# Modulation sums of the first quarter on TensorE in 32-column tiles, and the second half of the features in two quarters

## The chip, the cores and the metric

One core of a Trainium2 chip runs the whole program. The metric is the device time in microseconds (us) of one execution. The kernel before was timed in three runs: 2482.34, 2482.88 and 2483.24 us, median 2482.88.

## The reference, cut to what matters

Three transformer-like layers over 256 tokens of 2048 features, in float32. Only the head of the first one is touched:

```
mod = silu(c) @ ada_w + ada_b            # c: 2048, ada_w: 2048 x 6144
shift, scale, gate = split(mod, 3)
h = rms_norm(x, norm_g) * (1 + scale) + shift
proj = h @ w_in                          # 256 x 2048 by 2048 x 9296
...
x = x + gate * mix
```

So no product of `h` can start before the shift and the scale of its features are there, and these are sums over all 2048 rows of a 50 MB matrix.

## The kernel before, in words

**Products.** Every large product runs over slabs: a slab is 1 MB of weights (two blocks of 128 rows by 1024 columns), fetched in two halves of 512 KB by SyncE's queue into one of five `raw` slots (RING = 5), rounded by ScalarE to `hi` (four slots, L1206) and completed by VectorE with `lo = raw - hi` (L1753). TensorE takes three passes for each block (hi·h_hi, lo·h_hi, hi·h_lo; L642 to L644), 24 matmuls of 512 columns for each slab. In what follows p0, p1, ... are the products of slabs 0, 1, ...; the order is a list written out by hand (`slabs`, L287 on), and every engine walks it in its own loop over m. SyncE fetches slab m when p(m-5) is done. Features are blocks of 128, 16 in all. p0 to p7 use blocks 0 to 3 (the first quarter), p8 to p15 blocks 4 to 7 (the second), p16 to p23 blocks 0 to 7 again for two other column groups, p24 to p27 blocks 8 to 15 (two to a slab), p28 and p29 are small ones over all 16. In step m of the loops over the front (L1385, L2060) ScalarE and VectorE first hand over finished PSUM banks, then convert slabs up to m + 3 (`conv_to(m + 3)`), and then do whatever else is put at that step.

**Modulation.** `ada_w` comes in 48 slabs a of 1 MB: a = 0 to 7 and 8 to 15 hold the shift and the scale columns of the first and the second quarter, 16 to 23 the shift columns of the second half, 24 to 31 its scale columns, 32 to 47 the gate's. VectorE multiplies each by silu(c) and adds it to a row of 1024 sums on every partition, two instructions a slab (L1729, L1732); slab 1 alone is taken by TensorE, by 16 matmuls with one moving column (L786). When eight slabs are summed, TensorE sums over the partitions and turns the result into columns by matmuls against a column of ones (`quarter_columns` L768, `ada_columns` L743), VectorE adds bias and gain (`quarter_scales` L1829, `modulation` L1820), ScalarE writes `h_raw` and `h_hi` (L1251, L1253) and VectorE `h_lo` (L1817), two feature blocks in one `split_modulated(i)`; it raises `h_ready` by 2, and a product waits for `h_ready` up to its last block.

**Order of the sums.** `conv(m)` of VectorE first does the ada slabs up to `ada_until(m)` (L307, L1762): for m from 8 to 24 one slab to each step, so that the last one (a = 31) stands ahead of conv(24), and a gate slab ahead of conv(25), conv(26), conv(27), ... The columns of the second half are made inside p21 and p22, its scales in VectorE's step 22 (T_COLS), `split_modulated(4)` and `(5)` in step 22, `(6)` and `(7)` in step 23. POOL's queue fetches a from 13 on, each when VectorE is done with an earlier one (L2506), and a = 0 to 12 stand in SyncE's queue between the first slabs (L550 to L571).

**Start.** x (2 MB) comes by ScalarE's queue; its normalised rows xn are turned by TensorE (`turn_xn`, L755), four times four blocks ahead of the first columns and four times four behind them, ahead of p0.

Of the kernel before, what the change touches and what calls it, by code (L numbers as in the profile page):

```python
# [12 lines left out]
P = 128  # L13
# [81 lines left out]
def build(nc, t_in, out):  # L95
# [33 lines left out]
    def slot(i):  # L129
        return G0 + 8 * i  # L130
# [4 lines left out]
    gate = at("gate", [P, D], slot(7))  # L135
    ada_sum = [gate[:, 0:GW], gate[:, GW:D], tmp1, tmp2, gate[:, 0:GW], gate[:, GW:D]]
    ang = at("ang", [P, 4, TT * 96], G0 + 83)
# [160 lines left out]

    ADA_COLS = (0, HALF, GW, D + GW, 2 * D, 2 * D + GW)
    N_ADA, N_MOD, N_QUARTER, N_START = 48, 32, 8, 16  # L300
    PE_ADA = (1,)

# [4 lines left out]
    def ada_until(m):  # L307
        gates = sum(t <= m for t in GATE_AT)
        return N_MOD + gates if gates else (6, 8, 10, 11, 12, 13, 14, 15)[m] if m < 8 else min(N_START + m - 8, N_MOD)

# [203 lines left out]
    def ada_part(a, part):  # L514

        k, c = 2 * (a % 8) + part, ADA_COLS[a // 8]
        dst = ada_slot(a)[:, part * GW:(part + 1) * GW]
        if a >= N_START:
            return ada_w[k * P:(k + 1) * P, c:c + GW], dst
        both = ada_w[k * P:(k + 1) * P, 0:2 * D].rearrange("p (e n) -> p e n", e=2)  # L520
        return both[:, :, c:c + HALF], dst.rearrange("p (e n) -> p e n", e=2)
# [6 lines left out]
    def _(sp):  # L528
# [23 lines left out]
        for m in range(N_SLABS):  # L552
# [9 lines left out]
            if m == 3:  # L562
                sp.wait_ge(xn_ready, 2)
                ada_fetch(10, quarter_landed[2])
                sp.wait_ge(ada_added, added(7))
                ada_fetch(11, early_landed[2])
            if m == 4:
                sp.wait_ge(ada_added, added(8))
                ada_fetch(12, early_landed[3])
# [23 lines left out]
    def _(pe):  # L593
# [146 lines left out]

        columns_made = [0]

        def ada_columns():  # L743


            e, half = columns_made[0] // 2, columns_made[0] % 2
            pe.wait_ge(ada_added, added(8 * (2 + e + 1)))
            for k in range(4 * half, 4 * half + 4):
                ins = pe.matmul(wk[:, 2 + e, k:k + 1], ada_sum[2 + e][:, k * P:(k + 1) * P], ones[:, 0:1],
                                start=True, stop=True)  # L750
            if half:
                ins.then_inc(ada_turned, 1)
            columns_made[0] += 1

        def turn_xn(i):  # L755
# [11 lines left out]

        def quarter_columns(block, banks, start):  # L768

            pe.wait_ge(ada_added, added(8 * (block + 1)))  # L770
            for pair in range(2):
                for e in range(2):
                    for f in (2 * pair, 2 * pair + 1):
                        ins = pe.matmul(quarter_col(banks, e, f), ada_sum[block][:, e * HALF + f * P:e * HALF + (f + 1) * P],
                                        ones[:, 0:1], start=start, stop=True, skip_group_check=not start)
                ins.then_inc(ada_turned, 1)

        pe.wait_ge(c_silu, 1)
        pe.wait_ge(gains_out, 1)
        for a in PE_ADA:  # L780
            ada_wait(pe, a)
            for e in range(2):
                for f in range(4):
                    for part in range(2):
                        b = part * GW + e * HALF + f * P
                        ins = pe.matmul(quarter_col(acc, e, f), ada_slot(a)[:, b:b + P], c_col[:, 2 * a + part:2 * a + part + 1],  # L786
                                        start=a == PE_ADA[0] and f % 2 == 0 and part == 0, stop=False, skip_group_check=True)
            ins.then_inc(ada_taken, 1)
        pe.wait_ge(xn_ready, TT)
        for i in range(4):  # L790
            turn_xn(i).then_inc(turned, 1)
        quarter_columns(0, acc, False)
        for i in range(4, 8):
# [3 lines left out]
        def second_columns():  # L797

            pe.wait_ge(xn_parked, 8)
            quarter_columns(1, wk, True)  # L800

# [129 lines left out]
        for m in range(N_FRONT):  # L931
            if m == T_SECOND:
                product(*slabs[m], (0,))
                second_columns()
                product(*slabs[m], (1,))
            else:
                product(*slabs[m], range(TT), ada_columns if m in (T_COLS - 1, T_COLS) else None)
            if m == T_IK - 1:
# [252 lines left out]
    def _(act):  # L1191
# [51 lines left out]
        def split_modulated(i):  # L1243

            act.wait_ge(xn_parked, i + 1)
            act.wait_ge(mod_ready, (1, 2, 3, 4, 5, 5, 5, 5)[i])
            if i >= 2:
                act.wait_ge(h_ready, 2 * (i - 1))
            for k in (2 * i, 2 * i + 1):
                src = xnT[:, :, k, :]  # L1250
                act.activation(h_raw[:, k % 4].rearrange("p (t c) -> p t c", t=TT), src, ACT.Identity,  # L1251
                               bias=sh[:, k:k + 1], scale=gs[:, k:k + 1])
                act.activation(h_hi[:, :, k, :], src, ACT.Identity,  # L1253
                               bias=sh[:, k:k + 1], scale=gs[:, k:k + 1]).then_inc(h_hi_made, 1)
# [130 lines left out]
        for m in range(N_FRONT):  # L1385
# [21 lines left out]
            if m == T_LB + 1:  # L1407
                act.wait_ge(lb_ready, 1)
                act.activation(lb_col[:], lb_col[:], ACT.Exp).then_inc(lb_exp, 1)
            if m in (T_COLS, T_COLS + 1):  # L1410
                i = 4 + 2 * (m - T_COLS)
                split_modulated(i)
                split_modulated(i + 1)
# [296 lines left out]
    def _(vec):  # L1710
# [108 lines left out]

        def modulation():  # L1820

            c, shift_cols, scale_cols, signal = slice(8, 16), wk[:, 2, 0:8], wk[:, 3, 0:8], 5
            vec.wait_ge(ada_turned, signal)
            step(vec.tensor_tensor(sh[:, c], shift_cols, gcols[:, B_SHIFT, c], ALU.add))
            vec.wait_ge(ada_turned, signal + 1)
            step(vec.tensor_tensor(gs[:, c], scale_cols, gcols[:, B_SCALE, c], ALU.add))
            vec.tensor_tensor(gs[:, c], gs[:, c], gcols[:, N_MIX, c], ALU.mult).then_inc(mod_ready, 1)

        def quarter_scales(q, pair, banks):  # L1829

            vec.wait_ge(ada_turned, 2 * q + pair + 1)
            c = slice(4 * q + 2 * pair, 4 * q + 2 * pair + 2)
            vec.tensor_tensor(sh[:, c], banks[:, 2 * pair, 0:2], gcols[:, B_SHIFT, c], ALU.add)
            for f in range(2):
                k = 4 * q + 2 * pair + f
                ins = vec.tensor_scalar(gs[:, k:k + 1], banks[:, 2 * pair + 1, f:f + 1], gcols[:, B_SCALE, k:k + 1],
                                        gcols[:, N_MIX, k:k + 1], ALU.add, ALU.mult)
            ins.then_inc(mod_ready, 1)
# [6 lines left out]


        vec.wait_ge(rows_turned, 1)
        vec.tensor_copy(c_col[:], acc[:, 1, 0:KT]).then_inc(cols_out, 1)
        step(vec.tensor_copy(lb_col[:], acc[:, 1, KT:2 * KT]))
        vec.wait_ge(c_silu, 1)  # L1850
        ada_to(1)
        vec.wait_ge(rows_turned, 2)
# [207 lines left out]
        for m in range(N_FRONT):  # L2060
# [550 lines left out]
```

## Time and profile before

| | us |
|---|---|
| median of three runs | 2482.88 |
| the profiled execution | 2482.34 |
| its span in the trace | 2480.5 |
| TensorE matmul busy | 2435.8 (98%) |
| VectorE busy | 1625.9 (66%) |
| ScalarE busy | 1190.5 (48%) |
| DMA | 507 MB, 204 GB/s on average |

The profiled execution is 1.8 us longer than its span, and 0.5 us below the median. An engine's share is its busy time over the span. In the first fortieth (62 us) TensorE is busy for half of the time, in all the others for at least nine tenths; over the first 150 us the DMA engines move about 380 GB/s, later about 190.

### The profile page before, as it was taken

The numbers are of one execution on the slowest core, as the hardware profiler recorded it, in microseconds if no ns is written. First come the engines' busy times: TensorE is split into PE (matmuls) and PEld (weight loads), VectorE is DVE, ScalarE is ACT, GpSimd is POOL, SyncE is SP. The second block draws the span as 40 slices with busy tenths as digits, with TensorE's granted clock in tenths as the row PEclk, the third lists the DMA queues.
The fourth block names the chain that finished last, engine by engine and source line by source line (L and its number), as shares of the span: only waits on it lengthen the run. The fifth ranks groups of instructions, "written<-read, shape, count | busy, mean of one in ns | idle before, by whom it ended". The sixth has DMA issues, their size and how long they took to land.

```text
span 2480.5 us, 28566 instructions
## 1 busy us (share of the span) xinstructions
PE 2435.8 (98%) x11262; PEld 2016.7 (81%) x11262; DVE 1625.9 (66%) x2086; ACT 1190.5 (48%) x1549; POOL 110.1 (4%) x158
## 2 busy tenths in 40 slices
PE   5999999999999999999999999999999999999998
PEld 4888778888788888888888888888888888888887
DVE  6987988756776675764445655765676766754444
ACT  4756666445544444444343544554544444444332
POOL 1210000000100000000000212000000000000000
PEclk9999999999999999999999999999999999999999
DMA  9997655564565655656555655446565655656553
GB/s 385 364 365 245 238 187 171 180 244 153 171 199 190 194 197 188 200 190 207 197 190 190 193 195 180 154 146 207 174 200 188 196 194 189 200 188 208 197 189 135
DMA packets 189492, 507.04 MB, mean 204 GB/s; under 512 B 17792, under 2 KB 18080, under 8 KB 188080
## 3 DMA queue, kind: packets, MB, share of 16 engines
q1 hardware_dynamic: 177008, 456.92, 55.0%
q0 software_dynamic: 11824, 46.14, 5.0%
q8 instruction: 90, 1.47, 0.2%
q10 hardware_dynamic: 528, 2.16, 0.2%
q14 instruction: 42, 0.34, 0.0%
HBM read 503.06 MB, written 2.10 MB: 204 GB/s over the span
## 4 chain that ended last, share of the span: by engine, by line
PE 94%; DVE 4%; ACT 1%; issue 1%; DMA 1%; SPq 0%; DVEq 0%; ACTq 0%
PE acc L642 30%; PE acc L644 30%; PE acc L643 30%; DVE lo L1753 1%; DVE gate L1732 1%; PE wk L665 1%; DVE lo L1755 1%; DMA raw<-in_ada_w 1%; ACT hi L1206 0%; PE wk L1128 0%; PE wk L1154 0%; PE wk L826 0%; PE wk L1115 0%; PE wk L865 0%; PE wk L840 0%
## 5 line engine op out<-in xcount | busy, mean ns | idle before, releaser
L642 PE MATMUL acc<-hi,h 128*128 128x512 f32 x2592 | 1018.8, 393 | 3.6 <-ACT kiT L1322 1.5
L644 PE MATMUL acc<-hi,h 128*128 128x512 f32 x2592 | 1009.6, 390 | 0.0
L643 PE MATMUL acc<-lo,h 128*128 128x512 f32 x2592 | 1009.1, 389 | 0.0
L1755 DVE SCALAR_TENSOR_TENSOR lo<-raw,gcols,hi 128x1024 fp32r<-128x1024 f32 (+1 forms) x464 | 572.9, 1278 | 200.3 <-ACT hi L1206 198.3
L1206 ACT ACTIVATE hi<-raw,gcols 128x1024 fp32r<-128x1024 f32 (+1 forms) x464 | 497.4, 1128 | 361.5 <-PE acc L644 320.2
L1753 DVE TENSOR_TENSOR lo<-raw,hi 128x1024 fp32r<-128x1024 f32 (+1 forms) x388 | 453.5, 1213 | 301.3 <-ACT hi L1206 300.6
L642 PEld LDWEIGHTS acc<-hi,h 128*128 128x128 f32 x2592 | 486.8, 188 | 106.9 <-issue 5.4
L644 PEld LDWEIGHTS acc<-hi,h 128*128 128x128 f32 x2592 | 486.6, 188 | 102.0
L643 PEld LDWEIGHTS acc<-lo,h 128*128 128x128 f32 x2592 | 487.0, 188 | 98.9 <-issue 0.2
L1206 ACT ACTIVATE hi<-raw 128x1024 fp32r<-128x1024 f32 (+1 forms) x388 | 384.9, 1045 | 348.2 <-DMA raw<-in_w_ffn_down 164.7
L642 PE MATMUL acc<-hi,g_hi 128*128 128x512 f32 x704 | 274.2, 389 | 0.0
L644 PE MATMUL acc<-hi,g_lo 128*128 128x512 f32 x704 | 273.9, 389 | 0.0
L643 PE MATMUL acc<-lo,g_hi 128*128 128x512 f32 x704 | 273.9, 389 | 0.0
L644 PEld LDWEIGHTS acc<-hi,g_lo 128*128 128x128 f32 x704 | 132.1, 188 | 27.6
L642 PEld LDWEIGHTS acc<-hi,g_hi 128*128 128x128 f32 x704 | 132.1, 188 | 27.5
L643 PEld LDWEIGHTS acc<-lo,g_hi 128*128 128x128 f32 x704 | 132.2, 188 | 27.0
L2340 DVE STREAM_TRANSPOSE g_raw<-gated 32x256 f32<-32x256 f32 x320 | 139.6, 436 | 5.9
L2330 DVE SCALAR_TENSOR_TENSOR gated<-acc,stats,gated 128x512 f32<-128x512 f32 x44 | 33.0, 750 | 142.2 <-PE acc L644 142.2
L1598 ACT ACTIVATE gated<-acc,stats 128x512 f32<-128x512 f32 x44 | 30.3, 689 | 143.1 <-PE acc L644 143.1
L1232 ACT ACTIVATE h<-wk 128x512 fp32r<-128x512 f32 x44 | 24.4, 593 | 50.8 <-PE wk L665 50.4
L1800 DVE TENSOR_TENSOR h<-wk,h 128x512 fp32r<-128x512 f32 x44 | 28.8, 685 | 30.0 <-ACT h L1232 29.8
L1611 ACT ACTIVATE g_hi<-g_raw 128x512 fp32r<-128x512 f32 x40 | 23.1, 625 | 49.6 <-DVE g_raw L2340 49.6
(327 smaller groups left out, 1225.1 us busy)
## 6 DMA issues: line engine op xcount, KB each, us to landing
raw<-in_w_ffn_gate SPq DMA_DIRECT2D x176, 512.0 KB, 3.8
raw<-in_w_ffn_up SPq DMA_DIRECT2D x176, 512.0 KB, 4.6
raw<-in_w_ffn_down SPq DMA_DIRECT2D x176, 512.0 KB, 4.8
raw<-in_w_in SPq DMA_DIRECT2D x144, 512.0 KB, 4.7
raw<-in_w_kv SPq DMA_DIRECT2D x64, 512.0 KB, 4.8
ada_raw<-in_ada_w POOLq DMA_DIRECT2D x38, 512.0 KB, 7.7
gate_raw<-in_ada_w POOLq DMA_DIRECT2D x32, 512.0 KB, 5.6
raw<-in_w_out SPq DMA_DIRECT2D x32, 512.0 KB, 5.0
```

The source lines that it names most:

```text
L642: pe.matmul(o, l_hi, w_hi[:, c], start=first, stop=False, skip_group_check=loaded)
L643: pe.matmul(o, l_hi, w_lo[:, c], start=False, stop=False, skip_group_check=loaded)
L644: mm = pe.matmul(o, l_lo, w_hi[:, c], start=False, stop=last, skip_group_check=loaded)
L665: ins = pe.transpose(wk[:, i % 4, kk * P:(kk + 1) * P], block_of(4 * q + kk, t), ident[:])
L1206: ins = act.activation(hi[:, m % HI_SLOTS, c], raw[:, r, c], ACT.Copy, scale=scale)
L1598: act.activation(gated[:, t, :], acc[:, st.bank(t, 0), :], ACT.Silu, scale=rstd[:, t:t + 1]).then_inc(acc_free[st.bank(t, 0)], 1)
L1732: ins = vec.scalar_tensor_tensor(out=dst[:], in0=src, scalar=c_col[:, k:k + 1], in1=dst[:], op0=ALU.mult, op1=ALU.add)
L1753: ins = vec.tensor_tensor(lo[:, r, c], raw[:, r, c], hi[:, m % HI_SLOTS, c], ALU.subtract)
L1755: ins = vec.scalar_tensor_tensor(out=lo[:, r, c], in0=raw[:, r, c], scalar=gcols[:, st.gain, k:k + 1], in1=hi[:, m % HI_SLOTS, c], op0=ALU ...
L1800: vec.tensor_tensor(part_lo[:, t, k, :], wk[:, i % 4, :].rearrange("p (k c) -> p k c", k=4), part_hi[:, t, k, :], ALU.subtract).then_inc(h ...
L2330: vec.scalar_tensor_tensor(out=gated[:, t, :], in0=acc[:, st.bank(t, 1), :], scalar=rstd[:, t:t + 1], in1=gated[:, t, :], op0=ALU.mult, op ...
L2340: ins = vec.transpose(dst, src)
```

## The change

TensorE sums a = 0 to 7. silu(c) is written into column 0 of 16 groups of 32 columns of zeros (`c_pad`); for each ada slab four matmuls of 128 rows, 32 stationary and 512 moving columns go to the four 32-column tiles of the array, so that the four pieces (shift and scale of two row blocks) land on partitions 0, 32, 64 and 96 of one PSUM bank and accumulate over the eight slabs. ScalarE copies the bank (`ada_rows`), and four matmuls against a 0/1 selector of two columns make the columns of shift and scale. Slabs 0 to 4 come ahead of the first four turns of xn, slabs 5 to 7 behind them. VectorE has no ada slab before a = 8.

The second half is split as the first was: a = 16 to 23 hold shift and scale of blocks 8 to 11, a = 24 to 31 those of blocks 12 to 15 (fetched as 2 x 512 columns where it was 1024). Their columns are made in p21 and in p23, 8 matmuls each (before: 16 in p21 and p22); the scales stand in VectorE's steps 22 and 24; `split_modulated(4)`, `(5)` in step 22, `(6)`, `(7)` in step 24, behind conv(27). From m = 16 on `ada_until` is one slab lower: nothing ahead of conv(16), a = 30 ahead of conv(24), a = 31 and 32 ahead of conv(25).

```diff
+    c_pad = at("c_pad", [P, KT, 32], slot(7))
+    ada_rows = at("ada_rows", [P, HALF], slot(7) + 2)
-    ADA_COLS = (0, HALF, GW, D + GW, 2 * D, 2 * D + GW)
+    ADA_COLS = (0, HALF, 2 * HALF, 3 * HALF, 2 * D, 2 * D + GW)
-    PE_ADA = (1,)
+    PE_ADA = tuple(range(N_QUARTER))
@@ ada_until
-        return N_MOD + gates if gates else (6, 8, 10, 11, 12, 13, 14, 15)[m] if m < 8 else min(N_START + m - 8, N_MOD)
+        return N_MOD + gates if gates else (8, 8, 10, 11, 12, 13, 14, 15)[m] if m < 8 else min(N_START + m - 8 - (m >= N_START), N_MOD)
@@ SyncE, m == 3 and m == 4
-                sp.wait_ge(ada_added, added(7))
+                wait_summed(6)
-                sp.wait_ge(ada_added, added(8))
+                wait_summed(7)
@@ TensorE
+        def pair_columns(block, banks, pair):
+            pe.wait_ge(ada_added, added(8 * (block + 1)))
+            if block == 3:
+                pe.wait_ge(mod_ready, 5 + pair)
+            for e in range(2):
+                for f in (2 * pair, 2 * pair + 1):
+                    ins = pe.matmul(quarter_col(banks, e, f), ada_sum[block][:, e * HALF + f * P:e * HALF + (f + 1) * P],
+                                    ones[:, 0:1], start=True, stop=True)
+            ins.then_inc(ada_turned, 1)
...
+        def ada_row_sums(a):
+            ada_wait(pe, a)
+            for j in range(4):
+                ins = pe.matmul(acc[32 * j:32 * j + 32, 3, :], c_pad[:, 2 * a + j // 2, :],
+                                ada_slot(a)[:, j * HALF:(j + 1) * HALF], start=a == 0, stop=a == N_QUARTER - 1)
+            ins.then_inc(ada_taken, 1)
+        def first_columns():
+            pe.wait_ge(rows_out, 1)
+            pe.wait_ge(sel_ready, 1)
+            for pair in range(2):
+                for f in range(2):
+                    c = 2 * pair + f
+                    ins = pe.matmul(acc[:, 2 * pair, 2 * f:2 * f + 2], ada_rows[:, c * P:(c + 1) * P], sel,
+                                    start=True, stop=True)
+                ins.then_inc(ada_turned, 1)
-        for a in PE_ADA:
...
+        for a in range(5):
+            ada_row_sums(a)
         pe.wait_ge(xn_ready, TT)
         for i in range(4):
             turn_xn(i).then_inc(turned, 1)
-        quarter_columns(0, acc, False)
+        for a in range(5, N_QUARTER):
+            ada_row_sums(a)
+        first_columns()
@@ front loop
-                product(*slabs[m], range(TT), ada_columns if m in (T_COLS - 1, T_COLS) else None)
+                product(*slabs[m], range(TT), pairs_of(2 + (m > T_COLS)) if m in (T_COLS - 1, T_COLS + 1) else None)
@@ ScalarE
-            act.wait_ge(mod_ready, (1, 2, 3, 4, 5, 5, 5, 5)[i])
+            act.wait_ge(mod_ready, i + 1)
+        act.activation(c_pad[:, :, 0], c_col[:], ACT.Silu)
+        act.wait_ge(ada_taken, N_QUARTER)
+        act.activation(ada_rows[:], acc[:, 3, :], ACT.Copy).then_inc(rows_out, 1)
-            if m in (T_COLS, T_COLS + 1):
-                i = 4 + 2 * (m - T_COLS)
+            if m in (T_COLS, T_COLS + 2):
+                i = 4 + m - T_COLS
@@ VectorE
-        ada_to(1)
-        ada_to(3)
-        ada_to(N_QUARTER)
-            if m == T_COLS:
-                modulation()
-            if m in (T_SECOND - 2, T_COLS, T_COLS + 1):
-                i = 2 if m == T_SECOND - 2 else 4 + 2 * (m - T_COLS)
+            if m in (T_COLS, T_COLS + 2):
+                q = 2 + (m > T_COLS)
+                quarter_scales(q, 0, wk)
+                quarter_scales(q, 1, wk)
+            if m in (T_SECOND - 2, T_COLS, T_COLS + 2):
+                i = 2 if m == T_SECOND - 2 else 4 + m - T_COLS
```

## Rows read from the trace of the kernel before

**Rows 1.** Busy time by stretch: us, PE, PEld, DVE, ACT, POOL, PEclk, DMA share, GB/s.
```profile
0.00:45.00 45.00, 17.54 (x79) 16.69 (x80) 24.54 (x40) 16.97 (x20) 0.20 (x4) 1.00 0.97 374
45.00:80.00 35.00, 35.00 (x155) 29.07 (x154) 34.03 (x30) 22.87 (x34) 11.05 (x18) 1.00 1.02 391
...
260.00:2480.00 2220.00, 2206.95 (x10202) 1824.90 (x10201) 1410.82 (x1815) 1030.99 (x1297) 75.41 (x92) 1.00 0.57 189
```

**Rows 2.** Timeline, 38 to 47 us: start, duration, engine, line, [idle before].
```profile
38.85 3.57 PE L774 MATMUL acc<-ones,gate 128*128 128x1 f32 x16 [8.09 <-DVE gate L1732]
40.75 0.16 DVE L1833 TENSOR_TENSOR sh<-acc,gcols 128x2 f32<-128x2 f32 x1 [1.96 <-PE acc L774]
...
42.28 3.65 PE L760 MATMUL wk<-ident,xn 128*128 128x128 f32 x16
...
43.55 0.69 DVE L1817 TENSOR_TENSOR h<-h_raw,h 128x512 fp32r<-128x512 f32 x1 [0.56 <-ACT h L1253]
...
45.59 0.78 PE L642 MATMUL acc<-hi,h 128*128 128x512 f32 x1
```

**Rows 3.** SyncE's issue of early_raw, and its time to landing.
```profile
DMA to landing us min/median/max: 10.6/11.6/12.6
```

**Rows 4.** Timeline of TensorE around other float32 matmuls.
```profile
447.21 1.99 PE L894 MATMUL wk<-r_qe,r_e 128*32 128x64 f32 x128
537.01 3.60 PE L1011 MATMUL wk<-gate,ones 128*128 128x512 f32 x8
164.47 0.95 PE L749 MATMUL wk<-ones,tmp 128*128 128x1 f32 x8
```

**Rows 5.** Timeline of ScalarE, where it waited for slabs 4 and 7.
```profile
59.56 2.01 ACT L1206 ACTIVATE hi<-raw 128x1024 fp32r<-128x1024 f32 x2 [1.75 <-DMA raw<-in_w_in]
74.84 2.01 ACT L1206 ACTIVATE hi<-raw 128x1024 fp32r<-128x1024 f32 x2 [3.28 <-DMA raw<-in_w_in]
```

**Rows 6.** Timeline of VectorE and POOL, 48 to 88 us.
```profile
48.02 0.75 DVE L1729 TENSOR_SCALAR gate<-ada_raw,c_col 128x1024 f32<-128x1024 f32 x1
50.39 1.60 POOL L2509 DMA_DIRECT2D ada_raw<-in_ada_w  x2 [49.95 <-DVE gate L1732]
...
76.64 2.35 DVE L1753 TENSOR_TENSOR lo<-raw,hi 128x1024 fp32r<-128x1024 f32 x2
...
87.92 0.16 DVE L1833 TENSOR_TENSOR sh<-wk,gcols 128x2 f32<-128x2 f32 x1 [0.53 <-PE wk L774]
```

**Rows 7.** Timeline of VectorE, 159 to 198 us.
```profile
159.45 2.36 DVE L1753 TENSOR_TENSOR lo<-raw,hi 128x1024 fp32r<-128x1024 f32 x2 [0.52 <-ACT hi L1206]
...
171.30 2.60 DVE L1732 SCALAR_TENSOR_TENSOR gate<-gate_raw,c_col,gate 128x1024 f32<-128x1024 f32 x2
173.81 2.35 DVE L1753 TENSOR_TENSOR lo<-raw,hi 128x1024 fp32r<-128x1024 f32 x2
...
186.63 2.36 DVE L1753 TENSOR_TENSOR lo<-raw,hi 128x1024 fp32r<-128x1024 f32 x2 [2.27 <-ACT hi L1206]
189.61 0.69 DVE L1817 TENSOR_TENSOR h<-h_raw,h 128x512 fp32r<-128x512 f32 x1 [0.62 <-ACT h L1253]
...
192.20 2.60 DVE L1732 SCALAR_TENSOR_TENSOR gate<-gate_raw,c_col,gate 128x1024 f32<-128x1024 f32 x2
194.72 2.35 DVE L1753 TENSOR_TENSOR lo<-raw,hi 128x1024 fp32r<-128x1024 f32 x2
```

**Rows 8.** Timeline of ScalarE, 177 to 186 us.
```profile
177.00 0.60 ACT L1251 ACTIVATE h_raw<-xnT,sh,gs 128x256 f32<-128x256 f32 x1 [2.97 <-issue]
...
180.96 0.57 ACT L1313 ACTIVATE proj<-acc 128x512 f32<-128x512 f32 x1
...
185.55 1.99 ACT L1206 ACTIVATE hi<-raw 128x1024 fp32r<-128x1024 f32 x2
```

**Rows 9.** Issues of SyncE's queue at the ends of p22 and p25.
```profile
177.97 0.98 SPq L582 DMA_DIRECT2D raw<-in_w_in  x2
...
194.32 0.81 SPq L582 DMA_DIRECT2D raw<-in_w_in  x2
```

More of the change, by code:

```diff
@@ L135, in build @@
     gate = at("gate", [P, D], slot(7))
-    ada_sum = [gate[:, 0:GW], gate[:, GW:D], tmp1, tmp2, gate[:, 0:GW], gate[:, GW:D]]
+    ada_sum = [None, gate[:, GW:D], tmp1, tmp2, gate[:, 0:GW], gate[:, GW:D]]
+    c_pad = at("c_pad", [P, KT, 32], slot(7))
+    ada_rows = at("ada_rows", [P, HALF], slot(7) + 2)
     ang = at("ang", [P, 4, TT * 96], G0 + 83)
@@ L220, in build @@
     ssd, dstd = stats[:, 160:176], stats[:, 176:192]
+    sel = stats[:, 250:252]
     lam_s, lam_e, nlam = stats[:, 192:194], stats[:, 194:196], stats[:, 196:197]
@@ L373, in build @@
     ada_added, ada_turned, mod_ready = sem("ada_added"), sem("ada_turned"), sem("mod_ready")
+    pad_clear, sel_ready, rows_out = sem("pad_clear"), sem("sel_ready"), sem("rows_out")
     hi_made = sem("hi_made")
@@ L517, in ada_part @@
         dst = ada_slot(a)[:, part * GW:(part + 1) * GW]
-        if a >= N_START:
+        if a >= N_MOD:
             return ada_w[k * P:(k + 1) * P, c:c + GW], dst
@@ L739, in _ @@
         pe.transpose(acc[:, 0, 0:P], rows[:], ident[:]).then_inc(rows_turned, 1)
[L741 to L753, printed above, removed]
         def turn_xn(i):
@@ L766, in quarter_col, with pairs_of, fill, quarter_columns @@
             return banks[:, b, f % 2:f % 2 + 1]
-        def quarter_columns(block, banks, start):
+        def pair_columns(block, banks, pair):
             pe.wait_ge(ada_added, added(8 * (block + 1)))
-            for pair in range(2):
[L772 to L775, printed above, removed]
+            if block == 3:
[5 more added lines that the diff above has]
+            ins.then_inc(ada_turned, 1)
+        def pairs_of(block):
+            left = [0, 1]
+            def fill():
+                pair_columns(block, wk, left.pop(0))
+            return fill
+        def quarter_columns(block, banks):
+            for pair in range(2):
+                pair_columns(block, banks, pair)
+        def ada_row_sums(a):
[12 more added lines that the diff above has]
+                                    start=True, stop=True)
                 ins.then_inc(ada_turned, 1)
@@ L779, in _ @@
         pe.wait_ge(gains_out, 1)
-        for a in PE_ADA:
[L781 to L788, printed above, removed]
+        for a in range(5):
+            ada_row_sums(a)
         pe.wait_ge(xn_ready, TT)
@@ L799, in second_columns @@
             pe.wait_ge(xn_parked, 8)
-            quarter_columns(1, wk, True)
+            quarter_columns(1, wk)
         fills = []
@@ L1270, in _ @@
         act.wait_ge(cols_out, 1)
+        act.wait_ge(pad_clear, 1)
+        act.activation(c_pad[:, :, 0], c_col[:], ACT.Silu)
         act.activation(c_col[:], c_col[:], ACT.Silu).then_inc(c_silu, 1)
@@ L1818, in split_modulated @@
                               h_hi[:, :, k, :], ALU.subtract).then_inc(h_ready, 2)
[L1820 to L1827, printed above, removed]
         def quarter_scales(q, pair, banks):
@@ L1832, in quarter_scales @@
             c = slice(4 * q + 2 * pair, 4 * q + 2 * pair + 2)
-            vec.tensor_tensor(sh[:, c], banks[:, 2 * pair, 0:2], gcols[:, B_SHIFT, c], ALU.add)
+            if q:
+                shift_cols, scale_cols = banks[:, 2 * pair, 0:2], banks[:, 2 * pair + 1, 0:2]
+            else:
+                by_kind = banks[:, 2 * pair, 0:4].rearrange("p (f e) -> p e f", e=2)
+                shift_cols, scale_cols = by_kind[:, 0, :], by_kind[:, 1, :]
+            vec.tensor_tensor(sh[:, c], shift_cols, gcols[:, B_SHIFT, c], ALU.add)
             for f in range(2):
                 k = 4 * q + 2 * pair + f
-                ins = vec.tensor_scalar(gs[:, k:k + 1], banks[:, 2 * pair + 1, f:f + 1], gcols[:, B_SCALE, k:k + 1],
+                ins = vec.tensor_scalar(gs[:, k:k + 1], scale_cols[:, f:f + 1], gcols[:, B_SCALE, k:k + 1],
                                         gcols[:, N_MIX, k:k + 1], ALU.add, ALU.mult)
@@ L1844, in row_scale @@
             vec.sem_inc(rstd_ready, 1)
+        vec.memset(c_pad[:], 0.0).then_inc(pad_clear, 1)
+        for j in range(4):
+            for e in range(2):
+                ins = vec.memset(sel[32 * j:32 * j + 32, e:e + 1], float(e == j % 2))
+        ins.then_inc(sel_ready, 1)
         vec.wait_ge(rows_turned, 1)
@@ L1849, in _ @@
         step(vec.tensor_copy(lb_col[:], acc[:, 1, KT:2 * KT]))
-        vec.wait_ge(c_silu, 1)
-        ada_to(1)
         vec.wait_ge(rows_turned, 2)
@@ L1860, in _ @@
         vec.sem_inc(rstd0_ready, 1)
+        vec.wait_ge(c_silu, 1)
         conv_to(0)
-        ada_to(N_QUARTER)
         quarter_scales(0, 0, acc)
```

## The prediction

> **What bounds the kernel now.** I read the busy time by stretch first, then TensorE's waits, then the timelines at the two places that the change touches. TensorE is the bound from 45 us on: 35.0 of 35.0 us busy to 80 us, 2207 of 2220 us behind 260 us [rows 1]. So a gain can come from the first 45 us alone, where it works for 17.5 us, and from there on the change can only keep the gain or lose it. Two things run close behind TensorE in 45 to 80 us: the DMA engines (share 1.02, 391 GB/s: full) and VectorE (34.0 of 35.0 us) [rows 1]. What ends last at the start is VectorE's sum: the first columns wait 8.1 us for it, begin at 38.85, the first pair reaches VectorE at 40.75, h_lo of the first blocks is done at 44.24, and p0 begins at 45.59, behind 16 turns of 3.65 us [rows 2].
>
> **The change, part by part.** The sum runs in the clock of the profiled execution of before: span 2480.5 us, its time 2482.34, 1.8 us around the span; the median of the runs is 0.5 us above that time.
>
> *Row sums.* Slab 7's last half is the last issue of its group, at 22.9 us, and lands 10.6 to 11.6 us later [rows 3]: about 33.7. VectorE has then still to do 5 us. A 512-column float32 matmul runs as two instructions of 0.43 us (eight in 3.60 us, less the last one's tail of 0.6) [rows 4]. Four of them one after the other are 3.4 us for a slab, while a slab lands every 2.6 us; all four tiles at once are 0.86 us. For the tiles the trace has a row: 64 products in 32-column tiles, 128 instructions of 64 and 32 columns, take 1.99 us [rows 4]. At 0.84 ns a column they would take 5.2 us in single file, so nearly three run at a time. Of the clock: eight one-column instructions take 0.95 us at 164 us, but 16 of them 3.57 us at 38.85 [rows 2, 4], so TensorE is at 1.2 GHz before p0 and at 2.4 after it, whatever the clock column says there. I take 1.7 us for a slab at the lower level, 0.9 at the upper. Slabs 5 to 7 stand behind turns that end at about 31.3: done at 34.7 (upper) to 36.4 (lower), I take 35.5. Then 0.6 for ScalarE's copy, 0.45 to 0.9 for the first pair of columns, 0.2 of handing over: VectorE has them at 36.9 where it was 40.75, 3.8 us earlier (2.9 to 4.9). The memsets, the second Silu and the selector lie ahead of the first landing and cost nothing; without that cover they are under 1 us. p0 gains 3.5 to 5.
>
> The Trainium skill, page "TensorE: Matmul & The Clock Gate", section "Part 3: Packing small matmuls", says that matmuls start and end in strict program order. A float32 product is two instructions on one tile here, and the second must wait for the first; in strict order every neighbour would then overlap by one instruction only, and a slab would be 4 x 0.43 = 1.7 us (3.4 at the lower clock). The 128 instructions of [rows 4] would be 2.6 us in that order and took 1.8 without the tail, so the trace speaks against it; what it would cost is a rival below.
>
> *What is left of it at p8.* Behind the start two chains must come earlier too. VectorE works without a pause from 48.02 to 87.4, then waits 0.5 us for the second quarter's columns [rows 6]. Its work is the same as before, so it can only come as early as its inputs. Slabs 4 and 7 are converted the moment they land, 59.56 and 74.84 [rows 5]: the DMA engines are full and the same bytes must pass first. From a landing it takes VectorE 3.4 us to the end of that slab's lo (1.0 for the first half of hi, 2.4 for lo), and from the end of lo 7 (78.99) to the scales 8.4 us [rows 6]. So the scales can't come before 74.8 + 3.4 + 8.4 = 86.6, where they came at 87.92. Slab 4 may even land later, since POOL's first fetch (50.39) waits for VectorE's a = 8 and so moves 3.8 us ahead into the same full engines: one more half slab, 1.3 us, ahead of slab 4 gives 86.9. TensorE has been ahead meanwhile and waits at p8 for h. Of the 3.5 to 5 us, 1.0 to 1.3 are left: I take 1.1. The bounds are 0 (slab 4 later by another microsecond) and 4.8 (landings move along).
>
> *Second half.* Here in the clock of before, the 1.1 taken off at the end. Total work on TensorE is equal: 16 products of two instructions, 3.8 us, before and after. Removing one ada slab ahead of conv(16) puts VectorE 2.5 us ahead; but at conv(22) it already waited 0.52 us for ScalarE [rows 7], so there the lead ends in a longer wait. Ahead of conv(25) stand now a = 31 and a = 32: 171.30 + 2.5 + 2.5, conv(25) 176.3 to 178.7, first scales 179.3; before, ScalarE could start on them at 177.0 [rows 7, 8]. Costs:
> - p23 began just ahead of the issue at 177.97 [rows 9]; now 1.9 us earlier (two bursts of 0.95 have left p22 [rows 4]), at 175.9, and comes to its first columns at 177.3. They wait for `mod_ready` 5, at 179.3: 2 us, with all of p23 queued behind. With the columns' own 1.9 and 5.45 of product, p24 begins at 185.3 (two products of 5.45 ahead of 194.1 before, 183.2).
> - ScalarE: splits 4 and 5 from 179.4 to 183.3, the hand-over of p23's banks 4.6 us (180.96 to 185.55 before) [rows 8], hi 26 from 187.9.
> - VectorE: lo 26 followed hi by 1.1 (186.63) [rows 7, 8], now 189.0 to 191.4. And here is the dear step: before, split 6 came straight behind it, at 189.61, done at 190.3. Now step 24 puts the gate slab (2.5) and conv(27) (2.35) first [rows 7], then the scales (0.6), then ScalarE's four activations (2.0, as 177.0 to 179.0), then h_lo (0.8): 191.4 + 2.5 + 2.4 + 0.6 + 2.0 + 0.8 = 199.7.
> - p26 needs blocks 12 and 13. Before it began at 194.1, just ahead of the issue at 194.32 [rows 9]; TensorE is there at 185.3 + 2 x 5.45 = 196.2 and waits 3.5 us, to 199.7.
>
> So p26 begins 5.6 us late. The bounds: 4.0 if VectorE keeps its lead to conv(24), 6.5 if a gate slab lands late as well. After p26 everything hangs on TensorE again and VectorE has time to spare, so I count nothing as won back; the low bound of that is 1.5 us.
>
> Sum: 2480.5 - 1.1 + 5.6 = 2485.0 of span, 2486.8 with what lies around it; from the median, 2482.88 + 4.5 = 2487.4. That is slower, by just under 0.2% (5.0 us), which is about what a measurement of this kernel tells from no change.
>
> **The rivals.**
> - *The start's gain lives.* If slabs 4 to 7 land as much earlier as TensorE runs ahead, 4.8 less remain against 5.6: 2483.7. For it: each of these fetches is issued at the end of a product. Against it: the full engines [rows 1]. Chance 0.15.
> - *Not slower.* The second half costs nothing, because the scales of the last quarter come before TensorE wants them. It decides at h_lo of blocks 12 and 13: by 194.1 on this clock, 5.6 us earlier than in my chain. Then 1.1 are won, 2481.8, or 4.8 with the rival above, 2478.1. For it: p24 and p25 give 10.9 us of cover. Against it: the chain of rows above has no slack in it. Chance 0.15, of which 0.05 for over 0.2% faster.
> - *Tiles in program order, at the lower clock.* Slabs 5 to 7 then end at 31.3 + 10.2 = 41.5, the scales come 2.7 us later than before, and all behind them: 2482.88 + 2.7 + 5.6 = 2491.2. Chance 0.12.
> - *The clock falls in the new waits.* Before, no long wait follows p0 (13 us idle in all behind 260 us [rows 1]); now TensorE waits some 2.4 us at p8 and 3.5 at p26. If the clock drops, the next products run at half speed: between 0.7 us (as long as it lasted at 45.59) and one slab's 5.4: 2488 to 2493. Chance 0.08. The Trainium skill, same page, section "Why this matters for your kernels", advises to keep long idle gaps out between bursts for this reason; no row here shows a fall after such a wait.
>
> **How the numbers follow.** The forecast has 0.50; its own range is 2484.5 to 2489.5 (start 0 to 1.5 kept, second half 4.0 to 6.5). Slower by over 0.2%, above 2487.9: 0.16 of the forecast, 0.11 of the tiles, 0.07 of the clock, 0.34. Faster by over 0.2%: 0.05. Within: 0.61. The range reaches down through the kept gain and part of the third case, and up to the tiles' lower end: 2480.5 to 2490.5.
>
> **What would show it.** Row sums of 0.9 to 1.8 us a slab, the last done by 36.4; 3.4 or more would be the tiles in order. First scales at 36 to 38, p0 at about 41. Slab 4 landing at 59.5 to 61. A wait of TensorE for ScalarE or VectorE at about 88, and the second quarter's scales at 86.5 to 87.5. A wait of 1.5 to 2.5 us at p23's first columns, on VectorE's scales. A wait of 2.5 to 4.5 us at p26 on h_lo, right behind conv(27) and split 6 of VectorE. If the waits at p8 and p26 are both missing, the forecast is wrong; with p8's alone missing it is too slow by 3.7 us.

## The result, and the profile after

| | before | after |
|---|---|---|
| median of six runs, us | 2483.47 (2482.34 to 2484.08) | 2497.03 (2496.04 to 2498.59) |
| profiled execution, us | 2482.34 | 2498.59 |
| its span, us | 2480.5 | 2496.8 |

The ratio is 1.0056, with an interval of 1.0044 to 1.0067. The change makes the kernel 13.6 us slower; 4.5 were forecast, and the time lies above the range. The page of the changed kernel, engines (busy us, share of the span, instructions):

```profile
PE 2446.3 (98%) x11286; PEld 2012.9 (81%) x11286; DVE 1611.0 (65%) x2090; ACT 1191.1 (48%) x1551; POOL 116.6 (5%) x158
```

TensorE is busy 10.5 us longer than before (2435.8): 1.4 us of that lie ahead of p0, where it has taken over VectorE's sums, and 9.1 between p0 and p28, where its work is the same. The table has the start of each product on TensorE, after minus before:

| p0 | p1 | p2 | p3 | p4 | p5 to p22 | p23 | p24 | p26 | p27 |
|---|---|---|---|---|---|---|---|---|---|
| -5.2 | -5.7 | -1.1 | +1.9 | +5.8 | +8.4 | +6.5 | +13.9 | +16.1 | +16.2 |

So the start is won (5.7 us at p1), lost again with 8.4 more by p5, and the second half adds 7.8. The changed kernel's timeline where the first columns are made (start, duration, engine, line, [idle before <- releaser]); it answers to [rows 2]. The first two lines are the row sums of one slab each, at the lower and at the upper clock by their lengths; the clock column has no record ahead of 31.3 us:

```profile
26.59 1.93 PE L786 MATMUL acc<-early_raw,c_pad 128*32 128x512 f32 x8 [3.14 <-DMA early_raw<-in_ada_w]
...
34.33 1.07 PE L786 MATMUL acc<-early_raw,c_pad 128*32 128x512 f32 x8 [0.69 <-DMA early_raw<-in_ada_w]
36.75 0.16 DVE L1851 TENSOR_TENSOR sh<-acc,gcols 128x2 f32<-128x2 f32 x1 [6.82 <-PE acc L797]
...
40.35 0.47 PE L646 MATMUL acc<-hi,h 128*128 128x512 f32 x1 [1.39 <-issue]
```

The first scales come at 36.75 where they came at 40.75. Next the changed kernel's busy time by stretch (columns as in [rows 1]; the seventh group is the granted clock):

```profile
0.00:45.00 45.00, 24.12 (x126) 11.56 (x127) 11.29 (x39) 21.81 (x30) 0.20 (x4) 1.00 0.96 372
45.00:80.00 35.00, 26.85 (x94) 21.07 (x93) 25.94 (x22) 15.82 (x21) 10.36 (x16) 0.80 0.96 360
56.00:62.00 6.00, 6.00 (x14) 4.68 (x15) 3.22 (x3) 1.23 (x3) 3.81 (x7) 0.50 1.02 417
72.00:79.00 7.00, 5.33 (x13) 4.20 (x14) 6.83 (x6) 6.77 (x10) 1.44 (x2) 0.52 0.67 267
188.00:195.00 7.00, 7.00 (x23) 5.84 (x24) 3.86 (x6) 6.31 (x13) 0.00 (x0) 0.52 0.42 167
```

And the same stretch of the kernel before, for the third of these lines:

```profile
56.00:62.00 6.00, 6.00 (x28) 4.96 (x27) 5.93 (x6) 3.06 (x4) 4.12 (x7) 1.00 1.03 420
```

From 45 to 80 us TensorE now stands for 8.2 us (35.00 - 26.85), where it had no idle time. In three stretches, two of them here and one at 188 us, it runs at 1.2 GHz (0.50 to 0.52 of the full clock): in 56 to 62 us it is busy all the time and does 14 instructions where it did 28. What it stood for in the first 400 us (waits: engine, line, releaser, us in total, times, longest):

```profile
PE acc L646 <- ACT proj L1335: 8.2, 2, 4.4
PE acc L646 <- DVE h L1839: 2.1, 1, 2.1
PE wk L765 <- DVE gs L1854: 2.1, 1, 2.1
```

The first line is the surprise: ScalarE's hand-over of finished banks (`proj`). Its timeline in the changed kernel shows why:

```profile
53.29 2.00 ACT L1224 ACTIVATE hi<-raw 128x1024 fp32r<-128x1024 f32 x2 [6.14 <-DMA raw<-in_w_in]
55.20 2.04 ACT L1335 ACTIVATE proj<-acc 128x512 f32<-128x512 f32 x4
...
65.22 2.01 ACT L1224 ACTIVATE hi<-raw 128x1024 fp32r<-128x1024 f32 x2 [7.99 <-DMA raw<-in_w_in]
...
71.04 2.00 ACT L1224 ACTIVATE hi<-raw 128x1024 fp32r<-128x1024 f32 x2 [3.81 <-DMA raw<-in_w_in]
72.95 2.04 ACT L1335 ACTIVATE proj<-acc 128x512 f32<-128x512 f32 x4
```

ScalarE works in order: it stands 6.1 us for slab 3 with the hand-over of p1's banks behind that conversion, and 8.0 and 3.8 us for slabs 4 and 5 with the hand-over of p3's banks behind them. TensorE's side of it, in the timeline:

```profile
55.92 0.76 PE L646 MATMUL acc<-hi,h 128*128 128x512 f32 x1 [4.41 <-ACT proj L1335]
```

The chain of waits, 50 to 75 us, tells the same of p4 (start, duration, step):

```profile
47.17 23.85 DMA raw<-in_w_in
72.00 1.04 ACT hi L1224
73.05 0.49 ACT proj L1335
73.67 0.76 PE acc L646
```

Slab 4 landed at 65.2, before at 59.56 [rows 5]. Slab 3 was late too, by 1.0 us (53.27 and 52.25). POOL's first fetches were issued at 46.41 (before 50.39 [rows 6]). Bytes by DMA queue from 52 to 55 us (packets, MB, share of the 16 engines), in the changed kernel, where q0 is POOL's queue and q1 carries SyncE's:

```profile
q0 software_dynamic: 225, 0.79, 64.8%
q1 hardware_dynamic: 229, 0.45, 38.5%
```

and in the kernel before:

```profile
q1 hardware_dynamic: 412, 1.14, 94.8%
q0 software_dynamic: 31, 0.13, 10.3%
```

Over 49 to 58 us (three such windows) SyncE's queue moved 0.84 + 0.45 + 0.47 = 1.76 MB after, 1.21 + 1.14 + 0.62 = 2.97 before. POOL's moved 1.98 MB after and 0.74 before, 1.24 more. The 1.21 MB that SyncE's queue is short of take 5.9 us at 205 GB/s, an estimate from the 0.61 to 0.66 MB in 3 us that this queue moves from 58 to 64 us, beside POOL's, in both kernels: slab 4's 5.7 us.

The two queues sent nearly equal numbers of packets (225 and 229; 211 and 213 from 55 to 58 us; 180 and 180 from 58 to 61), from 52 to 55 us POOL's of 3.5 KB and SyncE's of 2.0 KB, so POOL had 64% of the bytes there, though SyncE had issued slab 4's fetch at 43.9 us and POOL its first one at 46.4. The Trainium skill, page "DMA: Bandwidth & Descriptors", section "Queues, rings and completion order", says that each DMA engine goes round its queues packet by packet; the trace agrees, with those counts of its own packets. That SyncE's fetch was the older one did not help it here.

### The profile page after: what moved, and what is told of

Read it like the earlier page. It is cut to its first block, busy times and chain, and to the rows that moved or that the text cites. A ratio compares the mean times of both kernels' runs of the same rounds, so it can differ in the third digit from the quotient of the medians.

```text
span 2496.8 us, 28618 instructions
## 1 busy us (share of the span) xinstructions
PE 2446.3 (98%) x11286; PEld 2012.9 (81%) x11286; DVE 1611.0 (65%) x2090; ACT 1191.1 (48%) x1551; POOL 116.6 (5%) x158
## 4 chain that ended last, share of the span: by engine, by line
PE 92%; DVE 4%; DMA 1%; ACT 1%; SPq 1%; issue 1%; DVEq 0%; ACTq 0%
PE acc L646 29%; PE acc L648 29%; PE acc L647 29%; DVE lo L1775 1%; DMA raw<-in_w_in 1%; PE wk L669 1%; DVE lo L1777 1%; SPq L552 1%; ACT hi L1224 1%; DMA early_raw<-in_ada_w 0%; PE wk L1146 0%; PE wk L1172 0%; DVE tmp L1754 0%; PE wk L844 0%; SPq L586 0%
## 5 line engine op out<-in xcount | busy, mean ns | idle before, releaser
L1335 ACT ACTIVATE proj<-acc 128x512 f32<-128x512 f32 x55 | 32.1, 595 | 34.2 <-PE acc L648 32.3
```

The lines of the kernel that those rows point to most:

```text
L1335: act.activation(proj[:, FIRST_SEGS[4 + g if st is st_first else g], t, n * HALF:(n + 1) * HALF], o, ACT.Copy).then_inc(acc_free[b], 1)
```

## The experiments

Edits are against the changed kernel unless another is named; each was timed against the kernel before on its own chip (before: 2483.21 for e1 to e4, 2483.33 for e5 to e8, 2483.5 for e9 to e11). Starts of products are the experiment's profile minus that of before.

| | median us (range) | ratio, interval | p2 | p5 | p9 | p22 | p26 |
|---|---|---|---|---|---|---|---|
| e1_start_only | 2490.12 (2489.20 to 2490.55) | 1.0025, 1.0015 to 1.0036 | +0.3 | +7.7 | +7.7 | +7.7 | +7.7 |
| e2_second_only | 2491.14 (2488.95 to 2492.12) | 1.0030, 1.0018 to 1.0041 | +0.5 | +0.5 | +2.3 | +2.3 | +8.4 |
| e3_start_hold | 2484.78 (2483.36 to 2485.43) | 1.0005, 0.9996 to 1.0015 | -1.7 | +1.0 | +2.3 | +2.3 | +2.3 |
| e4_start_order | 2486.92 (2486.23 to 2488.90) | 1.0015, 1.0006 to 1.0025 | -4.4 | +6.3 | +6.3 | +6.3 | +6.3 |
| e5_start_hold_order | 2481.70 (2480.99 to 2483.52) | 0.9994, 0.9985 to 1.0003 | -4.8 | -4.8 | -0.9 | -1.1 | -1.1 |
| e6_after_warm | 2499.17 (2496.97 to 2499.44) | 1.0060, 1.0045 to 1.0075 | -0.1 | +8.2 | +8.2 | +8.2 | +13.8 |
| e7_second_nolag | 2488.55 (2485.56 to 2490.06) | 1.0019, 1.0010 to 1.0028 | +1.6 | +1.6 | +1.6 | +1.6 | +5.0 |
| e8_second_ahead | 2487.96 (2485.92 to 2488.97) | 1.0017, 1.0008 to 1.0026 | +0.2 | +0.2 | +1.1 | +1.2 | +3.4 |

**Which half costs what.** e1 keeps the new start and puts the second half back; e2 is the reverse.

```diff
-    ADA_COLS = (0, HALF, 2 * HALF, 3 * HALF, 2 * D, 2 * D + GW)
+    ADA_COLS = (0, HALF, GW, D + GW, 2 * D, 2 * D + GW)
...
-                product(*slabs[m], range(TT), pairs_of(2 + (m > T_COLS)) if m in (T_COLS - 1, T_COLS + 1) else None)
+                product(*slabs[m], range(TT), ada_columns if m in (T_COLS - 1, T_COLS) else None)
```

> The changed start (row sums in 32-column tiles) with the second half of the features as before. Theory T: POOL's fetches of a = 13 to 15 and of its small rows, released 4 us earlier, overtake the queue of slabs 3 to 5; ScalarE stands on these landings with the hand-over of the banks queued behind, TensorE waits twice (4.5 and 4 us) and its clock falls twice: p0 at 40.4, p6 at 87.2, and from there constant: about +8.4 us, 2492. Rival R (the loss lies in the second half, the start only delays it): p6 would still be late but the total would come out near 2484. Slab 4 lands at 65.

```diff
-    PE_ADA = tuple(range(N_QUARTER))
+    PE_ADA = (1,)
...
-        for a in range(5):
-            ada_row_sums(a)
+        for a in PE_ADA:
...
```

> The start as before, the second half in two quarters. By my prediction's chain: a wait of 2.0 at p23's columns and 3.5 at p26, +5.6 us, 2489. With the clock fall seen in the changed kernel (3.4 us lost in p23) the wait at p26 shrinks to about 2: +7.7 us, 2491. Rival (the two quarters cost something only because the start was late): no difference from before.

Alone the start costs 6.9 us and the second half 7.9; together that is 14.8, and the whole change 13.6. The longest waits of e1, then of e2:

```profile
PE acc L646 <- ACT proj L1348: 10.5, 2, 6.3
```

```profile
PE wk L785 <- DVE gs L1855: 2.1, 1, 2.1
PE acc L642 <- DVE h L1836: 2.1, 1, 2.1
```

e2's start is the old one; the 2.3 us that its profile has at p22 arose within p0 (0.5: the granted clock rises to its upper level at 47.5 us, where it was 46.5), at p6 (1.3, with a wait of 1.2 us for ScalarE's hand-over) and at p8 (0.4). So only its step from p22 to p26, 6.1 us, belongs to the second half.

**What holds ScalarE.** Two repairs of e1's kernel, each shown against it. e3 lets POOL's queue start its fetches from a = 13 on only once slab 4 has landed:

```diff
+        pool.wait_ge(raw_landed[4], 64)
```

> As e1, and POOL starts its fetches of a = 13 on only when slab 4 has landed. Theory T: slab 4 lands at 56 to 58 instead of 65, slab 5 at 60 to 63, p4 no longer waits; p2 still waits for the hand-over behind slab 3 (3 us) and the clock may fall once. 2481 to 2485. Rival R2 (the DMA engines are simply full, order does not matter): slab 5 still lands at about 70 and the time stays at 2492.

e4 has ScalarE convert one slab fewer in steps 0 and 2, so that the hand-overs of p1's and p3's banks no longer stand behind a conversion whose slab is late:

```diff
-                conv_to(m + 3)
+                conv_to(m + 3 - (m in (0, 2)))
```

> As e1, but ScalarE hands over the banks of p1 and p3 ahead of the conversion of slabs 3 and 5 (conv_to one lower in steps 0 and 2). Theory T: p2 follows p1 without a wait, at 51.4, and p4 waits for slab 4 itself (landing 65) to about 69 instead of 73.7; p6 at about 80 to 83 instead of 87.2: 2484 to 2488. If the queue on ScalarE is not what p2 waits for, nothing changes: 2492.

ScalarE in e3 (timeline), slabs 3, 4 and 5:

```profile
52.70 2.00 ACT L1237 ACTIVATE hi<-raw 128x1024 fp32r<-128x1024 f32 x2 [5.89 <-DMA raw<-in_w_in]
57.67 2.00 ACT L1237 ACTIVATE hi<-raw 128x1024 fp32r<-128x1024 f32 x2 [1.01 <-DMA raw<-in_w_in]
60.22 2.01 ACT L1237 ACTIVATE hi<-raw 128x1024 fp32r<-128x1024 f32 x2 [0.55 <-DMA raw<-in_w_in]
```

Slab 4 is there at 57.7 instead of 67.2 in e1, and of the two waits one is left, at p2, where slab 3 lands at 52.7 (before 52.25) though p1 starts 5.9 us earlier. e3's and e4's waits of TensorE:

```profile
PE acc L646 <- ACT proj L1348: 4.0, 1, 4.0
```

```profile
PE acc L646 <- DVE lo L1788: 8.1, 3, 7.3
```

In e4 p2 starts on time (-4.4), and p4 waits 7.3 us for slab 4 itself (landed 68.0). So the two causes are separate: order alone cures p2, the queue alone cures p4. Neither is enough to win anything: e3 is not told from no change, and e4 is slower. e5 has both edits:

> The changed start with both repairs: POOL held until slab 4 has landed, and ScalarE's hand-over ahead of conv(3) and conv(5). Theory T: p2 and p4 follow without waits and the clock stays up, so TensorE is 4 to 5 us ahead at p6; VectorE's chain to the second quarter's scales (slab 7's landing plus 11.8 us) then takes most of it back: 2480 to 2482. Rival: the wait only moves to p3 or p4 and the clock falls again: 2484 to 2486.

Its median is 1.6 us below that of before, which its interval does not tell from no change. Its profile shows TensorE 4.8 us early until p7; then it waits 2.8 at p8 for the second quarter, loses 1.0 more at half clock behind that wait, and 1.1 us are left from p10 on. Against e1's +7.7 the two repairs are worth 8.8 us together. VectorE there, in e5's timeline (the first line's fetch is a = 13, the last one is the second quarter's first scale):

```profile
67.70 2.60 DVE L1767 SCALAR_TENSOR_TENSOR gate<-ada_raw,c_col,gate 128x1024 f32<-128x1024 f32 x2 [0.47 <-DMA ada_raw<-in_ada_w]
...
86.04 0.15 DVE L1873 TENSOR_TENSOR sh<-wk,gcols 128x2 f32<-128x2 f32 x1
```

Between 82.43 and 86.1 VectorE makes the sines' tables. Against before (87.92 [rows 6]) the scales come only 1.9 us earlier.

**Is it the clock?** e6 is the whole change with 32 matmuls of 256 columns on idle operands ahead of p2:

```diff
+                if m == 2:
+                    pe.wait_ge(xn_parked, 8)
+                    for _ in range(32):
+                        pe.matmul(wk[:, 0, 0:T], h_hi[:, 0, 0, :], h_hi[:, :, 0, :], start=True, stop=True)
```

> The changed kernel with 32 idle matmuls of 256 columns into a free bank (results unused) in TensorE's wait ahead of p2, about 4 us of the 4.5. If the wait is what brings the clock down, it stays at 2.4 GHz through p2 and p3 and p4 begins at the same time (it waits for slab 5 anyway), so the total moves by 0 to 3 us: 2494 to 2497. If the clock falls regardless (for the missing DMA or another reason), the fall at 55 us stays.

Its windows and its wait:

```profile
56.00:62.00 6.00, 6.00 (x31) 5.00 (x30) 4.25 (x4) 2.28 (x5) 3.79 (x7) 1.00 1.03 419
70.00:78.00 8.00, 3.37 (x9) 2.76 (x10) 6.91 (x7) 6.00 (x9) 0.00 (x0) 0.57 0.82 331
```

```profile
PE acc L646 <- ACT proj L1339: 6.5, 1, 6.5
```

A miss: 2494 to 2497 was expected. The clock stays up through 56 to 62 us and p3 starts at +0.0 instead of +1.9, but p4 then waits 6.5 us instead of 3.8 for the hand-over behind slab 5, the clock falls during that wait, and p5 is at +8.2, in the changed kernel +8.4. So the wait at p2 is what brought the clock down there, and the 3 us that it cost were covered by slab 5's landing: the waits and the clock at p2 to p4 may not be priced one by one. The comparison is not quite clean, since slabs 3 and 5 each landed 1.0 us later than in the changed kernel (54.3 and 72.0). In the second half p23's wait of 2.1 us brought no fall this time, p26's wait was 3.2, and the clock fell there (p26 at +13.8, p27 at +16.8).

**The second half.** e7 is e2's kernel with the ada slabs at their old places; e8 is e2's kernel with the last quarter's scales and splits ahead of conv(27) on VectorE and ScalarE.

```diff
-        return N_MOD + gates if gates else (6, 8, 10, 11, 12, 13, 14, 15)[m] if m < 8 else min(N_START + m - 8 - (m >= N_START), N_MOD)
+        return N_MOD + gates if gates else (6, 8, 10, 11, 12, 13, 14, 15)[m] if m < 8 else min(N_START + m - 8, N_MOD)
```

> As e2, with the ada slabs a = 23 to 31 each one step earlier as before, so only the gate slab stands ahead of conv(25). By the prediction's chain the wait at p23's columns (2.1 us) and with it the fall of the clock go; the wait at p26 stays and grows to about 3.2, since TensorE comes earlier: 2486 to 2487. If the wait at p26 alone brings the clock down as well: 2488 to 2490.

```diff
+            if m == T_COLS + 2:
+                quarter_scales(3, 0, wk)
+                quarter_scales(3, 1, wk)
+                split_modulated(6)
+                split_modulated(7)
```

> As e2, with the last quarter's scales and splits 6 and 7 ahead of the gate slab and conv(27) on VectorE and ahead of conv(27) on ScalarE. By the chain the wait at p26 goes, the one at p23 (2.1) and its clock fall (1.7 to 3.4) stay: 2487 to 2489. If conv(27) was not what h_lo stood behind, the wait at p26 stays: 2491.

The waits, of e7 and of e8:

```profile
PE acc L642 <- DVE h L1836: 3.2, 1, 3.2
```

```profile
PE wk L785 <- DVE gs L1858: 2.1, 1, 2.1
```

Each edit removes exactly one of the two waits. e7 has none at p23 and 3.2 us at p26, and a half clock behind it; from p22 to p27 it loses 5.1 us. e8 has none at p26, 2.1 at p23 and no fall: from p22 to p26 it loses 2.3. The medians, 5.2 and 4.6 us above before, lie closer together; e8's profiled execution (2485.92) is its fastest run and e7's (2489.08) is not, so the profiles say where, the medians how much. e8's profiled run has a mean granted clock of 0.999 and its nine others 0.995 to 0.998, so some of them may have had the fall that the profiled one lacks; that is not shown.

**Versions that might win.** On e5: e9 makes the tables six steps later (step 11 instead of 5) and ScalarE's sines from them in step 12 instead of 10, e11 is as e9 but releases POOL at slab 3; e10 is e5 with the whole second half and e7's and e8's edits.

```diff
-    T_LB, T_SECOND, T_COLS, T_SINES, T_GAINS = 26, 7, 22, 10, 13
+    T_LB, T_SECOND, T_COLS, T_SINES, T_GAINS = 26, 7, 22, 12, 13
...
+            if m == 11:
+                tables()
             if m == T_SECOND - 2:
-                tables()
```

> As e5, with the angle tables (3.7 us of VectorE) moved from ahead of the second quarter's scales to step 11, and ScalarE's sines to step 12. Theory T: in e5 the 4.8 us that TensorE is ahead at p7 are lost at p8 to VectorE's chain, 3.7 us of which are the tables; with them gone the scales come at about 83, TensorE does not wait at p8, the clock does not fall there, and 4 to 4.8 us stay: 2478.5 to 2480. If the ada landings bound that chain instead, it stays at 2481.7.

```diff
-            i = 4 + 2 * (m - T_COLS)
+            i = 4 + m - T_COLS
...
+            if m == T_COLS + 2:
+                quarter_scales(3, 0, wk)
+                quarter_scales(3, 1, wk)
+                split_modulated(6)
+                split_modulated(7)
```

> The whole change with every repair: POOL held, the hand-over first, ada slabs a = 23 to 31 a step earlier, the last quarter's scales and splits ahead of conv(27). If e7 and e8 name all that the second half costs, it is then neutral: as e5, 2481 to 2483. If something else in the two quarters costs, 2484 or more.

```diff
-        pool.wait_ge(raw_landed[4], 64)
+        pool.wait_ge(raw_landed[3], 64)
```

> As e9, with POOL released one slab earlier, when slab 3 has landed (53 instead of 58). Theory T: the ada landings come 4 us earlier and slab 5 and 6 later, to about 66 and 70; TensorE needs slab 5 at 65 (p5 at 68.5 less 3.4), so this may bring a wait back: 2479 to 2482, not better than e9.

e9: 2481.18 (2479.46 to 2483.28), ratio 0.9990 (0.9982 to 0.9999), the fastest kernel here; its scales come at

```profile
83.83 0.15 DVE L1873 TENSOR_TENSOR sh<-wk,gcols 128x2 f32<-128x2 f32 x1
```

which is 2.2 us before e5's, and TensorE is 4.1 ahead at p8 to p13, without the wait at p8 and the fall behind it. From p14 on it is 1.9, below the 4 to 4.8 expected: ScalarE stands for the late tables with a hand-over behind its sines, the same trap again, and TensorE waits 1.9 us:

```profile
121.12 0.36 ACT L1440 ACTIVATE sine<-ang 128x192 f32<-128x192 f32 x1 [5.81 <-DVE ang L1934]
```

e10: 2482.34 (2480.22 to 2483.47), 0.9994 (0.9985 to 1.0003); the same 1.6 us ahead before and behind the second half, so the split in quarters, repaired, is worth nothing. e11: 2484.71 (2483.51 to 2486.37), 1.0005 (0.9996 to 1.0014), above the 2479 to 2482 expected, with a 2.2 us wait on ScalarE at p6 and one of 2.3 at p8: POOL's release at slab 4 matters. Of the versions that might win only e9 is told from no change, and barely.

## Why the prediction was wrong, by its own steps

**The sign was right, and the second half's mechanism; the start's was not.** On the profiles the start came out at +8.4 us for -1.1, 9.5 worse, and the second half at +7.8 for +5.6, 2.2 worse. The second half alone would have given the sign.

- *Row sums.* Right. 1.93 us a slab at the lower clock and 1.07 at the upper (I took 1.7 and 0.9, for 8 passes of 512 columns), first scales 36.75 for 36.9, p0 5.2 earlier for 3.5 to 5. The rival of tiles in strict order (0.12) wanted 3.4 us at the lower clock; 1.93 says that the four tiles run together, and it is out.
- *"One more half slab, 1.3 us, ahead of slab 4": the step that failed.* It had the cause, POOL's fetch moving 3.8 us ahead into full DMA engines, and priced it as one transfer in one line. Six of POOL's half slabs had landed when slab 4 did (the last at 64.8), before it one (58.2), with 64% of the bytes from 52 to 55 us, and slab 4 landed 5.7 us later instead of 1.3. e3 shows it: with POOL held, 57.7. (The 86.9 that the step arrives at does not follow from the numbers beside it either: 86.6 and 1.3 are 87.9, no gain at all.)
- *"TensorE has been ahead meanwhile and waits at p8".* That no wait comes before p8 was assumed and never looked up. [Rows 5] already had ScalarE waiting 1.8 us for slab 4 and 3.3 for slab 7; p0 4 to 5 us earlier needs the hand-over that much earlier, and it stands behind a conversion that can't move, because landings don't. I counted ScalarE as an engine with 48% busy. e4 and e5 show it: two steps of one slab less, and the wait at p2 is gone. The sign given at the end, that with p8's wait alone missing the forecast is too slow by 3.7 us, pointed the wrong way: that wait is missing in the changed kernel because TensorE comes to p8 8.4 us late.
- *The cap at p8.* Where the landings are mended, e5 keeps 1.1 us, as forecast, but that is luck: its scales come 1.9 us earlier, not 1.0, and 1.0 goes to the slow clock behind p8's wait. Its way there is another, too: a = 13, which is there only at 67.7, and from there VectorE without a pause up to the scales, the sines' tables included (e9), not slab 7.
- *Second half.* p23's wait: 2.1 us for 2.0, with p22's end 1.9 earlier as worked out. p26's: 2.1 for 3.5. p26 starts 7.7 us later against p22, not 5.6, because the clock fell behind p23's wait: 7 us at 0.52, 3.4 lost, which shortened p26's wait: 2.1 + 3.4 + 2.1 = 7.6. In e6 and e7, where the clock did not fall at p23, p26's wait is 3.2, close to the 3.5 forecast. The timeline of the changed kernel, where the clock fell behind a wait of 2 us:

```profile
187.93 1.50 PE L765 MATMUL wk<-ones,tmp 128*128 128x1 f32 x8 [2.08 <-DVE gs L1854]
```

Before, the same eight took 0.95 us [rows 4]. VectorE's order at p26 is the one of the prediction, to the instruction: gate slab, lo 27, then the split:

```profile
201.82 2.60 DVE L1754 SCALAR_TENSOR_TENSOR gate<-gate_raw,c_col,gate 128x1024 f32<-128x1024 f32 x2
204.34 2.35 DVE L1775 TENSOR_TENSOR lo<-raw,hi 128x1024 fp32r<-128x1024 f32 x2
209.40 0.69 DVE L1839 TENSOR_TENSOR h<-h_raw,h 128x512 fp32r<-128x512 f32 x1 [1.82 <-ACT h L1271]
```

- *The clock rival* had 0.08 and came true three times, for 9.1 us, as an addition to the forecast and not in its place. That was a second fault: the forecast had three new waits, of 2.4, 2.0 and 3.5 us, and a chance of a fall behind each. The rival named those at p8 and p26 and not the one at p23, which brought the fall that cost most. The Trainium skill, page "TensorE: Matmul & The Clock Gate", section "Why this matters for your kernels", warns of it; the traces of after, e1 to e7 agree with 0.50 to 0.60 behind their waits.
- *The kept gain* (0.15): landings did not move along; the other way round. *Not slower* (0.15): the scales of the last quarter came 2.1 us too late, not in time.

The sum as measured, on the spans: start -5.7; wait at p2 4.6 and slow clock 3.0; wait at p4 3.9 and slow clock 2.7; p23 2.1, clock 3.4, p26 2.1, and 0.2 of small ones: 16.3 = 2496.8 - 2480.5. e6 shows that the front's terms can't be taken out one at a time: without the slow clock at p2 the wait at p4 is 2.8 us longer, since the landing of slab 5 ends it.

Still open: why e2 lost 1.8 us at p6 to p8 in its profile and e8 0.9. Slab 7 landed at 77.9 and 77.1 there, before at 74.8. The one edit that reaches this stretch is the new form of the fetch of a = 16, issued at 72.3 in e2; e7 has it too, slab 7 landed at 76.1 there, and nothing was lost, so it may be chance. Open too is why the clock fell behind some waits of 2.1 to 2.3 us and not behind others. Nor was it tried to give p2's slab 3 an earlier fetch.

## What to carry to other kernels

When a stage is made faster ahead of a stretch in which the DMA engines are full, ask for every in-order engine in that stretch which instruction it will stand at and what is queued behind it: here the idle ScalarE (48% busy) held TensorE because a bank's hand-over stood behind a conversion of a slab that could not land earlier. Here a fetch released 4 us earlier in one queue took bandwidth from an older one in another, which landed 5.7 us later, so hold the less urgent queue back by an explicit wait on the urgent landing. And give every new wait of TensorE of 2 us or more the price of a stretch at half clock behind it (1.0 to 3.4 us each here) with a chance: in the profiles of these kernels, from p0 on, the clock fell with each of the eleven waits of 2.8 us or more, and with three of the eight of 2.1 to 2.3 us.

## What the runs showed of the hardware that was not expected

- The granted clock fell during or behind waits of 4.4 us (p2) and 3.8 (p4), 6.3 and 4.1 (e1), 4.0 (e3), 7.3 (e4), 2.8 (e5 and e10), 6.5 and 3.2 (e6) and 3.2 (e7). Of the waits of 2.1 to 2.3 us it fell behind those at p23 in the changed kernel and in e2, ahead of one-column matmuls, and at p8 in e11, and not behind those at p26 in the changed kernel and in e2, at p23 in e6 and e8 and at p6 in e11. e5's fall, in its busy time by stretch:

```profile
90.00:93.00 3.00, 3.00 (x8) 2.33 (x8) 2.18 (x3) 2.94 (x7) 0.00 (x0) 0.50 0.95 391
```

- Float32 matmuls on four 32-column tiles ran fully together: a slab's four, of two instructions each, are 8 x 512 columns in 1.07 us (in the trace four instructions start within 0.02 us and the other four 0.43 to 0.45 us behind them), where one 128 x 512 product alone takes 3.60 / 4 = 0.9 ([rows 4], eight instructions).
- 64% of the bytes went to the queue with the larger packets (3.5 KB against 2.0 KB) at equal packet counts.
